# Splitting half of the down projection's columns on GpSimd in a 64-expert MoE kernel

## The reference, cut to what matters

```python
g = jnp.einsum('sd,edf->sef', hs, w_gate)      # 1024 -> 256, per expert
u = jnp.einsum('sd,edf->sef', hs, w_up)
act = jax.nn.silu(g) * u * gs[:, :, None]
return jnp.einsum('sef,efd->sd', act, w_down)  # 256 -> 1024, per expert
```

## Time and profile before

| | |
|---|---|
| median of 3 runs | 1141.26 us (1138.83 to 1143.55) |
| profiled execution | 1139.13 us, span 1137.4 us |
| mean granted TensorE clock | 0.966 |
| TensorE busy | 1042.1 us, 92% |
| VectorE, ScalarE, GpSimd busy | 67%, 50%, 46% |

### The profile page before, as it was taken

The page is one execution under the profiler, slowest core; times in us unless marked ns, Lnnn a source line. Parts: engine busy times, 40 slices in busy tenths (PEclk is TensorE's granted clock), DMA queues, the critical chain, the costliest instruction groups (busy, mean ns, idle before and its releaser), DMA issues.

```text
span 1137.4 us, 14545 instructions
## 1 busy us (share of the span) xinstructions
PE 1042.1 (92%) x4500; PEld 725.2 (64%) x4500; DVE 761.9 (67%) x1282; ACT 568.2 (50%) x605; POOL 522.1 (46%) x222
## 2 busy tenths in 40 slices
PE   0699997979798999999999999999999999999975
PEld 0587775547663667766677667766677667666532
DVE  4649785652755677777777777777777777677247
ACT  4334135642341556655566556655566556655401
POOL 0233213540222466566655666566655666566300
PEclk9799998989998999999999999999999999999979
DMA  9756751202152599999999999999998889898296
GB/s 320 262 181 247 276 203 47 75 28 84 74 222 82 189 353 370 347 353 374 369 379 361 362 362 358 353 366 370 367 358 336 340 334 355 331 345 332 79 387 278
DMA packets 68903, 318.66 MB, mean 280 GB/s; under 512 B 18640, under 2 KB 19152, under 8 KB 41360
## 3 DMA queue, kind: packets, MB, share of 16 engines
q1 hardware_dynamic: 42096, 267.41, 61.4%
q0 software_dynamic: 23104, 47.50, 11.5%
q10 hardware_dynamic: 3680, 3.46, 1.0%
HBM read 317.25 MB, written 39.85 MB: 314 GB/s over the span
## 4 chain that ended last, share of the span: by engine, by line
PE 79%; DVE 9%; DMA 6%; issue 2%; ACT 2%; SPq 1%; ACTq 0%; DVEq 0%; POOLq 0%; POOL 0%
PE ps L1229 20%; PE ps L1210 11%; PE ps L1212 11%; PE ps L1211 11%; PE ps L942 8%; PE ps L993 7%; DMA yall<-y_rows 4%; PE ps L1143 2%; PE ps L1118 2%; DVE acc L1362 1%; DMA ada<-in_w_ada_dram 1%; PE ps L1049 1%; PE ps L1075 1%; PE ps L1163 1%; DMA hg<-h_rows,idxg 1%
## 5 line engine op out<-in xcount | busy, mean ns | idle before, releaser
L586 POOL DMA_INDIRECT hg<-h_rows,idxg x70 | 352.7, 5038 | 147.7 <-DVE idxg L1669 147.4
L1675 DVE TENSOR_TENSOR wlo<-raw,whi 128x2048 fp32r<-128x2048 f32 x134 | 300.6, 2285 | 0.0
L820 ACT ACTIVATE whi<-raw 128x2048 fp32r<-128x2048 f32 x136 | 261.4, 1923 | 0.1
L1229 PE MATMUL ps<-rawd,actt 128*128 128x512 f32 x544 | 244.5, 592 | 1.4 <-ACT actt L856 1.4
L1210 PE MATMUL ps<-whi,hthi 128*128 128x512 f32 x544 | 225.3, 414 | 0.0
L1212 PE MATMUL ps<-whi,htlo 128*128 128x512 f32 x544 | 213.0, 392 | 0.0
L1211 PE MATMUL ps<-wlo,hthi 128*128 128x512 f32 x544 | 212.8, 391 | 0.0
L1689 DVE TENSOR_TENSOR htlo<-ps,hthi 128x1024 fp32r<-128x1024 f32 x68 | 83.3, 1225 | 177.2 <-ACT hthi L852 177.2
L862 ACT ACTIVATE ysb<-ps 128x1024 f32<-128x1024 f32 x68 | 69.6, 1024 | 213.5 <-PE ps L1229 213.5
L1229 PEld LDWEIGHTS ps<-rawd,actt 128*128 128x128 f32 x544 | 102.8, 189 | 104.7 <-issue 97.8
L594 POOL DMA_INDIRECT y_rows<-ysb,idxs x68 | 73.2, 1076 | 161.1 <-ACT ysb L862 153.7
(11 more groups left out here) (247 smaller groups left out, 1283.0 us busy)
## 6 DMA issues: line engine op xcount, KB each, us to landing
raw<-in_w_gate_dram SPq DMA_DIRECT2D x68, 1024.0 KB, 7.6
raw<-in_w_up_dram SPq DMA_DIRECT2D x68, 1024.0 KB, 10.9
rawd<-in_w_down_dram SPq DMA_DIRECT2D x68, 1024.0 KB, 12.8
ada<-in_w_ada_dram SPq DMA_DIRECT2D x24, 1024.0 KB, 7.2
yall<-y_rows SPq DMA_DIRECT2D x8, 2048.0 KB, 24.3
wraw<-in_w_in_dram POOLq DMA_DIRECT2D x10, 1024.0 KB, 6.0
woraw<-in_w_out_dram SPq DMA_DIRECT2D x16, 256.0 KB, 2.7
xs<-in_x_dram SPq DMA_DIRECT2D x4, 512.0 KB, 10.8
```

The costliest lines, as they stand in the source:

```text
L586: gp.indirect_dma_start(out=hg[s][:, :, :].rearrange("p k q -> p (k q)"), out_offset=None, in_=h_rows, in_offset=bass.IndirectOffsetOnAxis ...
L820: A(whi[:, s, :, cols], raw[:, s, :, cols], ACT.Copy).then_inc(hi_ok, 1)
L1229: ins = mm(bank(4 + hf), actt[:, k, :], rawd[:, s, k, hf * 512:(hf + 1) * 512], start=(k == 0), stop=(k == KF - 1))
L1675: V.tensor_tensor(wlo[s][:, :, c0:c1], raw[:, s, :, c0:c1], whi[:, s, :, c0:c1].bitcast(F32), ALU.subtract).then_inc(lo_dve, 1)
```

## The change

The down product's columns are divided in two. Columns 512 to 1023 stay as they are, plain f32 (2 of the 4 matmuls). Columns 0 to 511 become a split product of fp32r matmuls, 6 for a block. For it GpSimd rounds the 2 x 512 columns into `dhi` (one buffer) and writes the rest, raw minus rounded, into `dlo`, which lies over `rawd` itself. ScalarE copies the activations twice (rounded into `acthi`, plain into `actt`), and VectorE subtracts the two (`actlo`). These three have two slots.

The down product of a block stands one block later on TensorE (b-2 at the end of block b), and with it the evacuation (b-4 in step b), the scatter and the refill of `rawd`.

```diff
+            def split_down(i, s):
+                gp.wait_ge(wd_in[s], i * 16 + 16)
+                if not (isinstance(i, int) and num(i, s) == 0):
+                    gp.wait_ge(dn_mm, num(i, s))
+                gp.sem_inc(split_go, 1)
+                gp.tensor_copy(dhi[:, :, :], rawd[:, s, :, 0:512]).then_inc(dhi_ok, 1)
+                gp.wait_ge(dhi_ok, num(i, s) + 1)
+                gp.tensor_tensor(dlo[:, s, :, 0:512], rawd[:, s, :, 0:512], dhi[:, :, :].bitcast(F32),
+                                 ALU.subtract).then_inc(dlo_ok, 1)
...
-                if late:
-                    scatter(*after(i, s, -3))
+                if late >= 4:
+                    scatter(*after(i, s, -4))
                 gather(*after(i, s, 2))
+                if late >= 2:
+                    split_down(*after(i, s, -2))
```

SyncE's refill, ScalarE and VectorE:

```diff
-                sp.wait_ge(dn_mm, num(*after(i, s, -3)))
-                load_down(e_down, s)
+            def refill_down(i, s, e):
+                sp.wait_ge(dn_mm, num(i, s) - 1)
+                load_down(e, s)
...
+                    refill(i, s, num(i, s))
+                    refill_down(*after(i, s, -3), num(*after(i, s, -3)))
...
-                A(actt[:, :, :], bank(3)[:, 0:F].rearrange("p (k q) -> p k q", k=KF), ACT.Copy).then_inc(actt_ok, 1)
+                A(acthi[:, s], rows, ACT.Copy)
+                A(actt[:, s], rows, ACT.Copy).then_inc(actt_ok, 1)
...
+            def act_low(i, s):
+                v.wait_ge(actt_ok, num(i, s) + 1)
+                V.tensor_tensor(actlo[:, s], actt[:, s], acthi[:, s].bitcast(F32), ALU.subtract).then_inc(actlo_ok, 1)
...
                 low(i, s, 0)
                 low(i, s, 1)
+                if late >= 2:
+                    act_low(*after(i, s, -2))
                 times_up(*after(i, s, -1))
```

TensorE:

```diff
             def acts_tr(i, s):
                 pe.wait_ge(act_ok, num(i, s) + 1)
+                if not (isinstance(i, int) and num(i, s) == 0):
+                    pe.wait_ge(actt_ok, num(i, s))
...
-                for hf in range(2):
-                    for k in range(KF):
-                        ins = mm(bank(4 + hf), actt[:, k, :], rawd[:, s, k, hf * 512:(hf + 1) * 512],
-                                 start=(k == 0), stop=(k == KF - 1))
+                for k in range(KF):
+                    mm(bank(5), actt[:, s, k, :], rawd[:, s, k, 512:D], start=(k == 0), stop=(k == KF - 1))
+                pe.wait_ge(dlo_ok, num(i, s) + 1)
+                pe.wait_ge(actlo_ok, num(i, s) + 1)
+                for k in range(KF):
+                    for n, (a, w) in enumerate(((acthi[:, s, k, :], dhi[:, k, :]),
+                                                (acthi[:, s, k, :], dlo[:, s, k, 0:512]),
+                                                (actlo[:, s, k, :], dhi[:, k, :]))):
+                        ins = mm(bank(4), a, w, start=(k == 0 and n == 0), stop=(k == KF - 1 and n == 2))
...
-                down(*after(i, s, -1))
+                if late >= 2:
+                    down(*after(i, s, -2))
...
             acts_tr(m + (E // 2 - 1), 1)
+            down(m + (E // 2 - 1), 0)
             down(m + (E // 2 - 1), 1)
```

More of the change, by code:

```diff
@@ L77, in block_kernel @@
         rawd = at("rawd", [P, SLOTS, KF, D], F32, 32 * KB)
+        dlo = at("dlo", [P, SLOTS, KF, D], F32R, 32 * KB)
+        dhi = at("dhi", [P, KF, 512], F32R, 116 * KB)
         whi = at("whi", [P, SLOTS, 2, 2048], F32R, 48 * KB)
@@ L164, in block_kernel @@
         act_s = small("act_s", [P, KF, P], F32)
-        actt = at("actt", [P, KF, P], F32, 184 * KB)
+        actt = at("actt", [P, SLOTS, KF, P], F32, 184 * KB)
+        acthi = at("acthi", [P, SLOTS, KF, P], F32R, 189 * KB)
+        actlo = at("actlo", [P, SLOTS, KF, P], F32R, 191 * KB)
         sht = at("sht", [P, 2, KF, P], F32, 64 * KB)
@@ L325, in block_kernel @@
         actt_ok = sem("actt_ok")
+        actlo_ok = sem("actlo_ok")
+        dhi_ok = sem("dhi_ok")
+        split_go = sem("split_go")
+        dlo_ok = sem("dlo_ok")
         dn_mm = sem("dn_mm")
@@ L463, in _, with refill @@
             load_gate_up(3, 1)
-            def refill(i, s, e, e_down):
+            def refill(i, s, e):
                 split_done(num(*after(i, s, -2)))
                 load_gate_up(e, s)
-                sp.wait_ge(dn_mm, num(*after(i, s, -3)))
-                load_down(e_down, s)
-            with sp.Fori(2, E // 2) as i:
+            def refill_down(i, s, e):
+                sp.wait_ge(dn_mm, num(i, s) - 1)
+                load_down(e, s)
+            refill(2, 0, 4)
+            refill(2, 1, 5)
+            refill_down(1, 0, 2)
+            with sp.Fori(3, E // 2) as i:
                 for s in range(SLOTS):
-                    refill(i, s, num(i, s), num(i - 1, s))
+                    refill(i, s, num(i, s))
+                    refill_down(*after(i, s, -3), num(*after(i, s, -3)))
             sp.wait_ge(over_ok, 1)
@@ L480, in _ @@
                         e = sp.value_load(eid[0:1, bass.ds(num(i, s), 1)], min_val=0, max_val=E - 1)
[L481 to L486, removed]
+                        refill(i, s, e)
+                        e = sp.value_load(eid[0:1, bass.ds(num(*after(i, s, -3)), 1)], min_val=0, max_val=E - 1)
+                        refill_down(*after(i, s, -3), e)
+            for i, s in ((m + (E // 2 - 2), 1), (m + (E // 2 - 1), 0), (m + (E // 2 - 1), 1)):
+                e = sp.value_load(eid[0:1, bass.ds(num(i, s), 1)], min_val=0, max_val=E - 1)
+                refill_down(i, s, e)
             for s in range(SLOTS):
@@ L596, in scatter, with step_pool @@
                                       bounds_check=last_routed, oob_is_err=False).then_inc(scattered[s], 16)
-            def step_pool(i, s, late=True):
-                if late:
-                    scatter(*after(i, s, -3))
+            def split_down(i, s):
[7 more added lines that the diff above has]
+                                 ALU.subtract).then_inc(dlo_ok, 1)
+            def step_pool(i, s, late=4):
+                if late >= 4:
+                    scatter(*after(i, s, -4))
                 gather(*after(i, s, 2))
+                if late >= 2:
+                    split_down(*after(i, s, -2))
             gp.wait_ge(wo_mm, TT)
@@ L617, in _ @@
             gather(1, 0)
-            step_pool(0, 1, late=False)
-            step_pool(1, 0, late=False)
+            step_pool(0, 1, late=1)
+            step_pool(1, 0, late=2)
             gp.wait_ge(over_ok, 1)
@@ L633, in _ @@
             gp.sem_inc(fill_ok, 1)
-            step_pool(1, 1)
+            step_pool(1, 1, late=3)
             m = gp.value_load(npair[0:1, 0:1], min_val=0, max_val=OVER // 2)
@@ L642, in _ @@
                         step_pool(i, s)
+            last = m + (E // 2 - 1)
+            scatter(m + (E // 2 - 2), 0)
+            split_down(last, 0)
             scatter(m + (E // 2 - 2), 1)
-            scatter(m + (E // 2 - 1), 0)
-            scatter(m + (E // 2 - 1), 1)
+            split_down(last, 1)
+            scatter(last, 0)
+            scatter(last, 1)
         @block.scalar
@@ L855, in act_rows @@
                 ac.wait_ge(at_tr, num(i, s) + 1)
-                A(actt[:, :, :], bank(3)[:, 0:F].rearrange("p (k q) -> p k q", k=KF), ACT.Copy).then_inc(actt_ok, 1)
+                rows = bank(3)[:, 0:F].rearrange("p (k q) -> p k q", k=KF)
+                A(acthi[:, s], rows, ACT.Copy)
+                A(actt[:, s], rows, ACT.Copy).then_inc(actt_ok, 1)
             def y_out(i, s):
@@ L864, in step_act @@
             def step_act(i, s, late):
-                if late >= 3:
-                    y_out(*after(i, s, -3))
+                if late >= 4:
+                    y_out(*after(i, s, -4))
                 ht_high(i, s)
@@ L910, in _ @@
             for b in range(3, 6):
-                step_act(b // 2, b % 2, 3)
+                step_act(b // 2, b % 2, b)
             with ac.Fori(3, E // 2) as i:
                 for s in range(SLOTS):
-                    step_act(i, s, 3)
+                    step_act(i, s, 4)
             ac.wait_ge(over_ok, 1)
@@ L919, in _ @@
                     for s in range(SLOTS):
-                        step_act(i, s, 3)
+                        step_act(i, s, 4)
             last = m + (E // 2 - 1)
-            y_out(m + (E // 2 - 2), 1)
+            y_out(m + (E // 2 - 2), 0)
             act_rows(last, 0)
             silu(last, 1)
+            y_out(m + (E // 2 - 2), 1)
+            act_rows(last, 1)
             y_out(last, 0)
-            act_rows(last, 1)
             y_out(last, 1)
@@ L1226, in down, with block_pe @@
                     pe.wait_ge(y_ok, num(i, s))
-                for hf in range(2):
-                    for k in range(KF):
-                        ins = mm(bank(4 + hf), actt[:, k, :], rawd[:, s, k, hf * 512:(hf + 1) * 512],
-                                 start=(k == 0), stop=(k == KF - 1))
+                for k in range(KF):
[7 more added lines that the diff above has]
```

(26 more changed lines are left out.)

## The result

The changed kernel takes 1185.45 us (median of 4 runs, 1173.24 to 1188.79); the kernel before took 1141.52 beside it. The ratio is 1.037 (95% interval 1.031 to 1.043): slower, where 1179 had been predicted. The profiled execution took 1184.96, with a span of 1183.2.

What follows compares the result with a forecast made beforehand. Exclusive GpSimd and VectorE work of 10.75 us a block was to bind, above TensorE's 9.90: 66 x (10.75 - 10.23) = +34, +4 for the ends, 1139.1 + 38 = 1177, as median 1179 us; range 1121 to 1214.

Steps and rivals of the forecast that it cites:

- TensorE at 9.90: TensorE's block after the change: 9.90 us in place of 10.23 if nothing else binds, at most 22 us gained.
- The transition that might have taken 0.1 us: On TensorE, one transition after plain matmuls: up to 0.1 us, which would leave 15 us of gain.
- Exclusion of GpSimd and VectorE: Two-input SBUF work of VectorE, GpSimd's subtraction and descriptor writing exclude each other for whole instructions; 10.75 us with the copy.
- rival 1: The split fits: the copy doesn't exclude VectorE, the scatter slips between split and VectorE's weight subtractions; 1123 us, chance 0.13.
- rival 4: VectorE's one-hot rows also wait for the split, +0.74, 11.5 us a block, 1228 us, or gathers land late; chance 0.15.
- The sum of 10.75 us in every block: VectorE's subtractions, scatter, gather, dispatch and GpSimd's split exclude each other: 10.75 us a block, above TensorE's 9.90.
- the ring: VectorE's weight subtractions, then scatter and gather, then GpSimd's split, with the next subtractions behind it: 10.75 us a block.
- the dispatch: On GpSimd, between the evacuation and the scatter's start: up to 0.85 us, half of it taken, 0.43.
- the late load: Down weights, landing 10.8 to 14.0 us after issue, are wanted at the start of the second block after it; no term.
- Ends of the stage: Start and end of the expert stage: up to 3.4 us earlier in front, 6 more at the end; +4 taken.

Runs made afterwards that it cites:

- the race is taken away: Changed kernel, but VectorE waits in front of its weight subtractions until GpSimd's split of the block is done: 1181.44 us, 1.0375.
- The best version: Changed kernel, but SyncE issues the down weights of a block before gate and up: 1131.9 us, 0.9945 to the kernel before.

## Why the prediction was right in the number and half wrong in the reason

- **TensorE at 9.90**: right, 9.87 measured when nothing else binds; the plain records stay at 0.59 us as shown and the split ones take 0.23 from start to start. The transition that might have taken 0.1 us shows no cost.
- **Exclusion of GpSimd and VectorE**: right, and harder than thought: it holds for the copy too. GpSimd's took 5.65 in place of 1.04 us beside VectorE's pair, and VectorE's small copy of `vcur` took 1.03 in place of 0.17 beside GpSimd's copy (at 871.89). So one of rival 1's two conditions was false. The one-hot rows stand behind the split as rival 4 has it, but no block became 11.5 us by that alone.
- **The sum of 10.75 us in every block**: the step that failed. Alone, the split takes 1.04 + 2.40 with 0.1 between, as priced (3.6). But scatter and gather were put into the ring at 2.3 us with the dispatch, and they don't belong there. In the short block above the scatter runs from 864.39 to 865.42 while VectorE's pair from 864.86 takes its usual 4.48, and the gather ends at 868.03, 1.3 us before that pair does. They may wait for VectorE; they don't hold it up. Without them the exclusive work is 4.49 + 0.35 + 3.6 = 8.4 us, under 9.90, and 39 of 66 blocks ran at the TensorE-bound period or near it. The dispatch itself is 0.31, not 0.43.
- **"I give the late load no term of its own"**: the other step that failed, and the place where the time went. The prediction had each link (late subtractions delay gate and up, and the down weights behind them) and set the whole to nothing, because a longer period would relieve the DMA queue. The relief came, a DMA share of 0.85 to 0.91 for 0.88 to 0.96, and didn't help: the time from issue to landing, 11 to 12 us, makes the copy some 2 us late, and the rest comes from the issue, which slips by up to 3.8 us. The links close to a loop of 21.5 us for two blocks, which the prediction did not add up. A slip in the sum made it look better: 0.33 + 10.8 - 10.75 is +0.4 and not -0.1, so the subtractions could start at +4.0 at the earliest, not at +3.5. Over 9.87 us, the 66 periods have 65 us too much: 46 in the nine long blocks, 8.5 in the seven blocks behind them that run in part at the lower clock (0.85 to 0.94 granted), 11 in the rest. Against that the faster product gave 66 x (10.26 - 9.87) = 26. The difference is the 39.5 us between 677.0 and 716.5.
- **Ends of the stage**: +4 was taken; measured 81.1 - 75.5 = 5.6 at the end (6 had been worked out) and 0.6 in front, where no gain came.
- **Why the number came out**: 34 us of ring that isn't there against 39.5 of stalls that had no term. The two are alike in size by chance; that the loop through the loads is 10.8 us a block is chance as well, since it is made of other terms. The expected profile, an even 10.4 to 11.2 us, was wrong; the profile shows 9.9 and 16.
- **The test named for the late load** ("wrong if GpSimd never waits for rawd") came out for it: GpSimd waits 90.7 us for it in 400.

Shown is that with the down weights earlier (by order, 1.037 to 0.994; by half the bytes, to 1.009) or the split elsewhere (0.998), all or most of the loss goes, and that it stays when the race is taken away and the loop is left (1.0375). What stays open is how the loss divides between the loop and loads that land late though issued in time, and how far the loads' pace could be raised; no run tried either. The best version has 10.00 us a block, so part of the 26 us of the split product was not got back.

## What to carry to other kernels

A load that was in time for its consumer is not in time for a new step in front of that consumer: list the deadline of each load, in the order in which the queue delivers them, and put the one with the earliest deadline first. Then follow what a late load delays until it comes back to that load's own issue, and add the loop up: if it is longer than the period, lateness grows until something stalls, even with DMA engines that have room. Where DMA is over 90% busy, as here, measure the loads' pace by shortening the bound engine before making that engine faster. A wait costs what stands behind it in the same engine's order (here scatter and gather, even with a split of 2x16 columns), and the mean period can hide that a stage is bimodal: look at single blocks.

## What the runs showed of the hardware that was not expected

- A one-input copy on GpSimd is blocked by VectorE's two-input subtractions as fully as a two-input one: 128x32 took 0.21 us alone and 4.20 beside them; 128x1024 1.04 and 5.65. It blocks VectorE in turn, even a copy of 128x24 (1.03 us in place of 0.17).
- Whether GpSimd gets in between two VectorE subtractions that follow each other varies. In the block at 446.25 its subtraction, issued 0.12 us after VectorE's first, took 4.36 us and VectorE's pair 6.63 in place of 4.48: it went in between. The copy at 607.40 did not and waited for both; the one at 521.35 did get in and took 1.42.
- A gather's descriptor writing waits for VectorE's subtractions, both of the pair or the first alone, and ends about 0.9 us behind (868.03, where the first of the pair, 2.28 us, ends at 867.14), but leaves the pair's time as it is (4.48 us), unlike a compute instruction.
- An idle stretch of TensorE of 4.2 us was followed by a granted clock of 0.50 in the rest of that block and of 0.87 over the next (11.33 us instead of 9.87).
